# A two-layer mixture-of-experts step: 64 rows per expert in layer 1, with both halves of x in one stationary operand, and w2 loaded in shorter runs

## The chip, the cores and the metric

The kernel runs on one core of one Trainium2 chip. The metric is the device time of one execution in microseconds (us), the median of several.

## What is computed

One inference step of a small streaming encoder: 384 token rows of 1024 (a prompt of 256 and 8 streams of 16) go through two layers. Layer 0 is a gMLP mixer and a mixture of experts, layer 1 latent attention and a mixture of experts. All values are fp32. The change concerns the experts, above all those of layer 1:

```python
def hier_moe(xn, w_group, b_group, w_expert, b_expert, w1, w3, w2):
    ...                                   # top-1 group, top-2 of its 4 experts: gates (384, 16)
    y = jnp.zeros_like(t)
    for e in range(N_EXPERTS):            # 16; w1, w3: 1024 x 512, w2: 512 x 1024
        hdn = jax.nn.silu(t @ w1[e]) * (t @ w3[e])
        y = y + gates[:, e:e + 1] * (hdn @ w2[e])
    return y.reshape(shp)
```

Each row goes to 2 of 16 experts, so an expert has 48 rows on average. With the reference's inputs the fullest has 66 rows in layer 0 and 62 in layer 1.

## The kernel before

**Stages.** gMLP until about 285 us, layer 0's experts from 285 to 553, attention from 553 to 790, layer 1's experts from about 805 to the end. The engines run programs of their own and meet at semaphores; each program is written out by hand, so its order is the code's.

**Rows and passes.** An expert takes CAP = 72 rows. What is over goes to an overflow loop at the end of the layer, of EXTRA = 10 passes that are skipped one by one when there is nothing over; SyncE, GpSimd, ScalarE and TensorE all run through it (`over`, `a.Fori(0, EXTRA)`).

**Precision.** A product of two fp32 operands is made from three: each operand is split into a high part (fp32r, rounded) and a low part (the rest), and high x high, low x high and high x low are summed in PSUM. `split_product` (L181) does so: 16 matmuls (L188) for 8 slices of 128 of the inner dimension, xh and xl in turn against the high part of the weight, then 8 (L194) of xh against its low part. A matmul streams 512 columns of the weight against a stationary slice of x of 128 x 72.

**One round of the loop** (`step`, for expert e; 16 rounds in each layer):

- SyncE loads w1, w3 and w2, 2 MB each, into six raw slots (`load`, L765). Load j of a layer waits until j - 5 weights have been used up (`w_used`). Each is one run of 16 KB in each of 128 partitions, "(p k) n", so slice k of the inner dimension is every 8th (w1, w3) or every 4th (w2) row.
- ScalarE makes a weight's high part (`moe_split_h`, L1079), VectorE the low one in place (`moe_split_l`, L1084).
- TensorE: `product_x` of w1 into bank BA, `transpose_hidden` of expert e - 1 (L1291), `product_x` of w3 into BB, `transpose_x` of the next expert (L1277), `product_y` of expert e - 1 with w2.
- ScalarE: silu of BA (L1133), `hidden_high` of e - 1 (L1100), a split, `x_high` of e + 1 (L1096), a split, `y_copy` of e - 1 (L1118), a split, and the issue of y's store (L1126).
- VectorE: `hidden_low` of e - 1 (L1185), a split, the product hidden = silu x BB (L1200), `x_low` of e + 1 (L1180), two splits. The output of L1200 is read and written by slices, since w2's slices are every 4th row. In layer 1 the table of kept rows (`keep_rows`, L1216 to L1232) comes after round 2 and `kept_columns` (L1236, L1237) after rounds 4 and 15.
- GpSimd fetches the rows of an expert from memory, two ahead (L866); expert 0's and 1's are gathered by TensorE instead (`gather_x`, L1308).

The two halves of x are kept twice (`xsplit`), for the present and the next expert.

Of the kernel before, what the change touches and what calls it, by code (L numbers as in the profile page):

```python
# [29 lines left out]
P = 128  # L30
# [23 lines left out]
CAP = 72  # L54
EXTRA = SLOTS // (CAP + 1)
# [47 lines left out]
def build(nc, A, O):  # L103

    top = ExitStack()
    with top:
# [564 lines left out]
        xsplit = [[sb(f"moe_x{p}{i}", [P, KD, CAP], F32R, moe) for p in "hl"] for i in range(2)]  # L671
# [44 lines left out]
        kept_y = low3[0:CAP, 0:2 * D].rearrange("q (e x n) -> q e x n", e=1, x=2)  # L716
# [13 lines left out]
        silu_done, hid_done = sem("silu_done"), sem("hid_done")  # L730
        hT_done, hh_ready, hl_ready = sem("hT_done"), sem("hh_ready"), sem("hl_ready")
# [27 lines left out]
        def moe_sync(sp, l):  # L759
# [43 lines left out]
            s = over[l]  # L803
# [3 lines left out]
            with sp.Fori(0, EXTRA) as i:  # L807
                with sp.If(n_over > i):
# [7 lines left out]
                    sp.dma_start(rows[0:CAP, 0, :], xrows[bass.ds(row, CAP), :]).then_inc(s["x"], 16)  # L816
# [4 lines left out]
                    sp.dma_start(yrows[bass.ds(row, CAP), :], rows[0:CAP, 2, :]).then_inc(s["st"], 16)  # L821
# [25 lines left out]
        def moe_pool(g, l):  # L847
            if l == 0:
# [67 lines left out]
        def route_vector(v, l):  # L916
            inverse_of_roots(v)
# [1385 lines left out]
```

## Time and profile before

| | |
|---|---|
| median of 3 runs | 1108.43 us (1107.47 to 1110.43) |
| the profiled execution | 1111.0 us, its span 1109.3 us |
| TensorE busy | 1055.8 us, 95% of the span |
| VectorE busy | 780.1 us, 70% |
| ScalarE busy | 595.1 us, 54% |
| DMA | 252 GB/s over the span, 374 to 405 GB/s in most slices of the experts' loops |
| mean granted clock of TensorE | 0.967 |

The chain of work that ended last is TensorE's by 86%, and L188 and L194, the products of the experts, are 46% of it. A granted clock of 1.00 is 2.4 GHz, 0.50 is 1.2 GHz. In a row of the profile, "<-" in square brackets names what ended the wait before an instruction.

### The profile page before, as it was taken

The page shows a single profiled execution, that of the slowest core. Times are in us where ns is not written, and L with a number is a line of the kernel's source. Part 1 is how long each engine was busy: PE and PEld are TensorE (multiplying, and loading weights), DVE is VectorE, ACT ScalarE, POOL GpSimd, SP SyncE. Part 2 cuts the span into 40 slices and gives each one's busy share as a digit, 9 for nine tenths or more (in the row PEclk, how much of TensorE's full clock was granted, in tenths as well). Part 3 has the DMA queues.
Part 4 walks back from the last instruction along what each step waited for, and adds up shares of the span by engine and source line. Part 5 has one row for each costly group of instructions (what it writes and reads, how often), then busy time and mean ns, then how long its engine had stood idle before and what let it go on. Part 6 is the DMA issues. An engine that isn't in the chain of part 4 may idle for free.

```text
span 1109.3 us, 13599 instructions
## 1 busy us (share of the span) xinstructions
PE 1055.8 (95%) x5197; PEld 768.2 (69%) x5197; DVE 780.1 (70%) x629; ACT 595.1 (54%) x462; POOL 84.9 (8%) x109
## 2 busy tenths in 40 slices
PE   5999999999999999999879998889999999999997
PEld 4889998797566666666567767776866666666664
DVE  4447654378698988989354648544678988988886
ACT  5245433253677777777333324232437777777770
POOL 5000000004000000000030020000030000000013
PEclk9999999989999999999989997888899999999999
DMA  9443432756799999997390013005379999999954
GB/s 350 145 162 133 163 128 100 310 240 253 277 396 385 380 400 390 403 387 317 88 337 14 2 39 152 1 1 242 137 287 374 377 387 385 386 402 389 405 198 171
DMA packets 44916, 279.88 MB, mean 252 GB/s; under 512 B 6392, under 2 KB 10904, under 8 KB 32184
## 3 DMA queue, kind: packets, MB, share of 16 engines
q1 hardware_dynamic: 33136, 240.21, 56.1%
q0 software_dynamic: 9216, 30.20, 7.9%
q10 hardware_dynamic: 2520, 8.85, 2.0%
q8 instruction: 32, 0.52, 0.2%
q14 instruction: 12, 0.10, 0.0%
HBM read 260.91 MB, written 18.50 MB: 252 GB/s over the span
## 4 chain that ended last, share of the span: by engine, by line
PE 86%; DVE 7%; ACT 3%; DMA 2%; issue 2%; ACTq 0%; SPq 0%; DVEq 0%
PE ps L188 31%; PE ps L194 15%; PE ps L526 4%; PE ps L580 4%; PE ps L623 3%; PE ps L1972 3%; PE ps L1997 2%; PE ps L586 2%; PE ps L534 2%; PE ps L630 1%; PE ps L1308 1%; PE ps L1068 1%; PE ps L1950 1%; PE ps L1277 1%; DVE moe_wl L1084 1%
## 5 line engine op out<-in xcount | busy, mean ns | idle before, releaser
L1084 DVE TENSOR_TENSOR raw_lo<-raw,moe_wh 128x4096 fp32r<-128x4096 f32 x48 | 212.4, 4425 | 43.9 <-ACT moe_wh L1079 43.9
L1084 DVE TENSOR_TENSOR moe_wl<-moe_raw,moe_wh 128x4096 fp32r<-128x4096 f32 x48 | 212.3, 4424 | 34.3 <-ACT moe_wh L1079 34.1
L188 PE MATMUL ps<-moe_wh,moe_xh 128*72 128x512 f32 x512 | 204.0, 398 | 5.1 <-DVE moe_xl L1180 4.8
L188 PE MATMUL ps<-moe_wh,moe_xl 128*72 128x512 f32 x512 | 202.2, 395 | 0.0
L1079 ACT ACTIVATE moe_wh<-raw 128x4096 fp32r<-128x4096 f32 x48 | 173.8, 3620 | 11.9 <-PE ps L2209 7.6
L1079 ACT ACTIVATE moe_wh<-moe_raw 128x4096 fp32r<-128x4096 f32 x48 | 173.7, 3621 | 4.0 <-DMA moe_raw<-in_moe_w_dram 4.0
L188 PEld LDWEIGHTS ps<-moe_wh,moe_xh 128*72 128x72 f32 x512 | 73.0, 143 | 49.4 <-DVE moe_xl L1180 5.7
L188 PEld LDWEIGHTS ps<-moe_wh,moe_xl 128*72 128x72 f32 x512 | 72.8, 142 | 43.2 <-issue 0.6
L328 DVE TENSOR_TENSOR raw_lo<-raw,gm_wh 128x4096 fp32r<-128x4096 f32 x12 | 53.1, 4425 | 69.7 <-ACT gm_wh L322 67.4
L188 PE MATMUL ps<-moe_wh,moe_hTh 128*72 128x512 f32 x256 | 81.9, 401 | 4.1 <-DVE moe_hTl L1185 3.3
L188 PE MATMUL ps<-moe_wh,moe_hTl 128*72 128x512 f32 x256 | 80.6, 396 | 0.0
L322 ACT ACTIVATE gm_wh<-raw 128x4096 fp32r<-128x4096 f32 x11 | 39.9, 3627 | 57.8 <-DMA raw<-in_gm_w_out_dram 29.1
L194 PE MATMUL ps<-moe_wl,moe_xh 128*72 128x512 f32 x272 | 68.7, 394 | 0.0
L1096 ACT ACTIVATE moe_xh<-ps 128x576 fp32r<-128x576 f32 x32 | 20.9, 652 | 79.7 <-PE ps L1277 53.1
L194 PE MATMUL ps<-raw_lo,moe_xh 128*72 128x512 f32 x240 | 60.6, 394 | 0.0
L1118 ACT ACTIVATE moe_rows<-ps 72x1024 f32<-72x1024 f32 x30 | 30.7, 1023 | 54.9 <-PE ps L194 54.9
L194 PEld LDWEIGHTS ps<-moe_wl,moe_xh 128*72 128x72 f32 x272 | 38.4, 141 | 24.6
L188 PEld LDWEIGHTS ps<-moe_wh,moe_hTl 128*72 128x72 f32 x256 | 36.6, 143 | 23.3 <-issue 0.8
L188 PEld LDWEIGHTS ps<-moe_wh,moe_hTh 128*72 128x72 f32 x256 | 34.3, 143 | 22.5 <-DVE moe_hTl L1185 3.6
L526 PE MATMUL ps<-gm_wh,gm_fx 128*128 128x512 f32 x192 | 46.3, 402 | 2.9 <-ACT gm_wh L315 2.9
L194 PEld LDWEIGHTS ps<-raw_lo,moe_xh 128*72 128x72 f32 x240 | 33.9, 141 | 21.6
L866 POOL DMA_DIRECT2D moe_rows<-moe_xrows x28 | 14.8, 527 | 420.5 <-PE ps L1277 384.9
(391 smaller groups left out, 1647.8 us busy)
## 6 DMA issues: line engine op xcount, KB each, us to landing
raw<-in_moe_w_dram SPq DMA_DIRECT2D x48, 2048.0 KB, 10.9
moe_raw<-in_moe_w_dram SPq DMA_DIRECT2D x48, 2048.0 KB, 11.1
raw<-in_gm_w_in_dram SPq DMA_DIRECT2D x7, 2048.0 KB, 8.0
moe_yrows<-moe_rows ACTq DMA_DIRECT2D x30, 288.0 KB
raw<-in_gm_w_out_dram SPq DMA_DIRECT2D x4, 2048.0 KB, 7.7
moe_rows<-moe_xrows POOLq DMA_DIRECT2D x28, 288.0 KB, 9.7
raw<-in_gm_w_in_dram SPq DMA_DIRECT2D x2, 1024.0 KB, 10.9
at_cache<-in_cache_ckv_dram SPq DMA_DIRECT2D x2, 1024.0 KB, 13.3
```

The costliest lines, as they stand in the source:

```text
L188: nc.tensor.matmul(out[c], x(t, k), wh[:, k, c * 512:c * 512 + 512], start=start and k == 0 and x is xh, stop=False)
L194: last = nc.tensor.matmul(out[c], xh(t, k), wl[:, k, c * 512:c * 512 + 512], start=False, stop=stop and k == nk - 1)
L322: nc.scalar.activation(w_gm[s][:], raw[:, s, :], ACT.Copy).then_inc(wh_ready, 1)
L328: nc.vector.tensor_tensor(raw_lo[:, s, :], raw[:, s, :], w_gm[s][:].bitcast(F32), ALU.subtract).then_inc(wl_ready, 1)
L526: nc.tensor.matmul(ps[:, 3 * (m % 2) + t], x_rows(x, k, t), wh[:, k], start=k == 0 and x is xth, stop=False)
L534: last = nc.tensor.matmul(ps[:, 3 * (m % 2) + t], x_rows(xth, k, t), wl[:, k], start=False, stop=k == KD - 1)
L580: nc.tensor.matmul(ps[:, u_bank(c), 0:TOK], wh[:, k, i * P:(i + 1) * P], x[:, k], start=k == 0 and x is xth, stop=False)
L623: nc.tensor.matmul(ps[:, 2 * t + c], x_rows(x, 4 * j + k, t), wh[:, k, c * 512:c * 512 + 512], start=j == 0 and k == 0 and x is uth, stop= ...
L1079: nc.scalar.activation(w_hi[hi][:], w_raw[slot], ACT.Copy).then_inc(wh_ready, 1)
L1084: nc.vector.tensor_tensor(w_lo[slot], w_raw[slot], w_hi[hi][:].bitcast(F32), ALU.subtract).then_inc(wl_ready, 1)
L1118: nc.scalar.activation(rows[0:CAP, 2 + par].rearrange("p (b n) -> p b n", b=2), ps[0:CAP, BY:BY + 2], ACT.Copy).then_inc(y_out, 1)
L1972: last = nc.tensor.matmul(ps[:, 2 + hp // 2, (hp % 2) * KC:(hp % 2 + 1) * KC], w_uk[:, s, hp * P:(hp + 1) * P], cTs[:, b, s], start=s == 0 ...
```

## The change

Layer 0 still takes 72 rows an expert, layer 1 takes 64, with 11 overflow passes in place of 10 (both layers). In layer 1 the two halves of x stand side by side in one stationary operand of 128 columns, `xwide`, the high half in the first 64, the low half in the other 64. One stacked matmul against the weight's high part does what two did: partitions 0 to 63 of the bank get xh's product, 64 to 127 get xl's. `stacked_product` takes 7 of these, 8 of xh against the low part, and the last stacked one. The two halves of the bank must then be added: ScalarE copies the upper half to SBUF (semaphore `moe_lower`), VectorE adds the lower one to it (`moe_summed`). The silu reads that sum, and the product reads two tiles of SBUF.

w2 is loaded in both layers as "(k p) n", four runs of 4 KB in a partition, and hidden stays in plain order, so L1200's strides are gone. SyncE issues `load_keys_up` (attention's w_uk) ahead of its wait for layer 0's overflow table. The semaphore `at_ms` is folded into `at_red`, with as many waits as before. `cap` replaces CAP wherever a layer's tile is cut.

```diff
-CAP = 72
-EXTRA = SLOTS // (CAP + 1)
+CAPS = (72, 64)
+CAP = max(CAPS)
+EXTRA = SLOTS // (min(CAPS) + 1)
...
+        xs = [sb(f"moe_x{i}", [P, 2 * KD * CAP], F32R, moe) for i in range(2)]
...
+        xwide = [x[:, 0:KD * P].rearrange("p (k t) -> p k t", k=KD) for x in xs]
...
-            return w.rearrange("o (p k) n -> p (o k) n", p=P)
+            return w.rearrange("o (k p) n -> p (o k) n" if name == "moe_w2" else "o (p k) n -> p (o k) n", p=P)
...
+            if l == 0:
+                load_keys_up(sp)
             sp.wait_ge(rt_table, l + 1)
...
             def step(e, par, m):                       # ScalarE
                 a.wait_ge(w_used, M_MOE[l] + (1 if is_first(e) else 3 * e))
                 at_least(a, hid_done, E0 + e)
-                nc.scalar.activation(sil[:], ps[0:CAP, BA], ACT.Silu).then_inc(silu_done, 1)
-                if not is_first(e):
+                if l:
+                    nc.scalar.activation(sil[0:cap], ps[cap:P, BA], ACT.Copy).then_inc(lower, 1)
+                    if not is_first(e):
+                        hidden_high(e - 1)
+                    moe_split_h(a, l, *([3, 0, 3, 0] if is_first(e) else [3 * e + 2, 2, 5 if par else 2, m]))
+                    a.wait_ge(w_used, M_MOE[l] + (2 if is_first(e) else 3 * e + 1))
+                    nc.scalar.activation(hid[0:cap], ps[cap:P, BB], ACT.Copy).then_inc(lower, 1)
+                    a.wait_ge(summed, 2 * e + 1)
+                nc.scalar.activation(sil[0:cap], sil[0:cap] if l else ps[0:cap, BA], ACT.Silu).then_inc(silu_done, 1)
...
             def step(e, par, m):                       # VectorE
+                if l:
+                    v.wait_ge(lower, 2 * e + 1)
+                    nc.vector.tensor_tensor(sil[0:cap], ps[0:cap, BA], sil[0:cap], ALU.add).then_inc(summed, 1)
                 if not is_first(e):
                     hidden_low(e - 1)
...
                 v.wait_ge(w_used, M_MOE[l] + (2 if is_first(e) else 3 * e + 1))
+                if l:
+                    v.wait_ge(lower, 2 * e + 2)
+                    nc.vector.tensor_tensor(hid[0:cap], ps[0:cap, BB], hid[0:cap], ALU.add).then_inc(summed, 1)
+                    v.wait_ge(summed, 2 * e + 2)
                 v.wait_ge(silu_done, E0 + e + 1)
-                nc.vector.tensor_tensor(hid[:].rearrange("q (k p) -> q k p", k=KE), by_slice(sil[:], KE), by_slice(ps[0:CAP, BB], KE),
-                                        ALU.mult).then_inc(hid_done, 1)
+                nc.vector.tensor_tensor(hid[0:cap], sil[0:cap], hid[0:cap] if l else ps[0:cap, BB], ALU.mult).then_inc(hid_done, 1)
...
+            def stacked_product(j, x, xh, wh, wl, bank):
+
+                pe.wait_ge(wh_ready, m0 + j + 2)
+                for k in range(KD - 1):
+                    nc.tensor.matmul(ps[:, bank], x[:, k], wh[:, k], start=k == 0, stop=False)
+                pe.wait_ge(wl_ready, m0 + j + 1)
+                for k in range(KD):
+                    nc.tensor.matmul(ps[0:cap, bank], xh[:, k], wl[:, k], start=False, stop=False)
+                return nc.tensor.matmul(ps[:, bank], x[:, KD - 1], wh[:, KD - 1], start=False, stop=True)
```

The order of VectorE in one round of layer 1 (expert 4), before: moe_hTl is the low part of hidden, raw_lo and moe_wl are low parts of weights, moe_xl that of x, moe_hidden the product.

```order
L1185 TENSOR_TENSOR moe_hTl<-ps,moe_hTh 128x288 [waits hh_ready]
L1084 TENSOR_TENSOR moe_wl<-moe_raw,moe_wh 128x4096 [waits wh_ready]
L1200 TENSOR_TENSOR moe_hidden<-moe_silu,ps 72x512 [waits silu_done,w_used]
L1180 TENSOR_TENSOR moe_xl<-ps,moe_xh 128x576 [waits xh_ready]
L1084 TENSOR_TENSOR moe_wl<-moe_raw,moe_wh 128x4096 [waits wh_ready]
L1084 TENSOR_TENSOR raw_lo<-raw,moe_wh 128x4096 [waits wh_ready]
```

And after, the same round:

```order
L1217 TENSOR_TENSOR moe_silu<-ps,moe_silu 64x512 [waits moe_lower]
L1205 TENSOR_TENSOR moe_hTl<-ps,moe_hTh 128x4x64 [waits hh_ready]
L1092 TENSOR_TENSOR moe_wl<-moe_raw,moe_wh 128x4096 [waits wh_ready]
L1224 TENSOR_TENSOR moe_hidden<-ps,moe_hidden 64x512 [waits moe_lower,w_used]
L1227 TENSOR_TENSOR moe_hidden<-moe_silu,moe_hidden 64x512 [waits silu_done,moe_summed]
L1200 TENSOR_TENSOR moe_x<-ps,moe_x 128x8x64 [waits xh_ready]
L1092 TENSOR_TENSOR moe_wl<-moe_raw,moe_wh 128x4096 [waits wh_ready]
L1092 TENSOR_TENSOR raw_lo<-raw,moe_wh 128x4096 [waits wh_ready]
```

One add has come ahead of hidden_low, one ahead of the product, each with a wait for ScalarE's copy (`moe_lower`).

The order of ScalarE in the same round, before:

```order
L1133 ACTIVATE moe_silu<-ps 72x512 [waits hid_done,w_used]
L1100 ACTIVATE moe_hTh<-ps 128x288 [waits hT_done]
L1079 ACTIVATE moe_wh<-raw 128x4096 [waits w_used,raw_loaded2]
L1096 ACTIVATE moe_xh<-ps 128x576 [waits xT_done]
L1079 ACTIVATE moe_wh<-raw 128x4096 [waits w_used,raw_loaded0]
L1118 ACTIVATE moe_rows<-ps 72x1024 [waits y_stored,w_used]
L1079 ACTIVATE moe_wh<-moe_raw 128x4096 [waits w_used,raw_loaded3]
```

And after, from the first copy (L1145) to the third split:

```order
L1145 ACTIVATE moe_silu<-ps 64x512 [waits hid_done,w_used]
L1111 ACTIVATE moe_hTh<-ps 128x4x64 [waits hT_done]
L1087 ACTIVATE moe_wh<-moe_raw 128x4096 [waits w_used,raw_loaded4]
L1150 ACTIVATE moe_hidden<-ps 64x512 [waits w_used]
L1152 ACTIVATE moe_silu<-moe_silu 64x512 [waits moe_summed]
L1107 ACTIVATE moe_x<-ps 128x8x64 [waits xT_done]
L1087 ACTIVATE moe_wh<-moe_raw 128x4096 [waits w_used,raw_loaded5]
L1129 ACTIVATE moe_rows<-ps 64x1024 [waits y_stored,w_used]
L1087 ACTIVATE moe_wh<-raw 128x4096 [waits w_used,raw_loaded1]
```

The silu (L1152) has moved from ahead of the round's first split to behind it and behind the copy of w3's upper half, and now waits for VectorE's first add.

## Rows read from the trace of the kernel before

**Rows 1.** stretches: start:end, length, busy time by engine, clock, DMA (columns first)
```profile
core 0: us, PE busy (x) PEld busy (x) DVE busy (x) ACT busy (x) POOL busy (x), PEclk, DMA share, GB/s
850.00:1040.00 190.00, 189.22 (x918) 118.95 (x917) 168.66 (x82) 141.98 (x75) 5.71 (x11) 1.00 1.00 389
949.15:966.58 17.43, 17.43 (x86) 10.95 (x84) 15.25 (x7) 13.12 (x7) 0.52 (x1) 1.00 1.01 391
949.00:954.00 5.00, 5.00 (x24) 3.04 (x23) 3.67 (x1) 4.34 (x2) 0.00 (x0) 1.00 0.99 315
954.00:961.00 7.00, 7.00 (x37) 4.44 (x36) 6.15 (x3) 4.61 (x4) 0.00 (x0) 1.00 1.02 433
144.00:148.00 4.00, 4.00 (x26) 4.00 (x25) 3.83 (x6) 1.55 (x2) 0.00 (x0) 1.00 1.00 404
544.76:548.17 3.41, 3.41 (x10) 1.90 (x9) 0.00 (x0) 0.00 (x0) 0.00 (x0) 0.50 0.83 228
581.30:590.00 8.70, 8.70 (x48) 7.74 (x48) 2.26 (x2) 2.18 (x4) 0.00 (x0) 1.00 0.27 72
```

**Rows 2.** chain of waits, layer 1's loop: start us, us, what
```profile
1042.16 0.25 PE ps L1291 x4
1042.41 3.72 PE ps L188 x16
...
1059.57 0.25 PE ps L1291 x4
```

**Rows 3.** landings: expert weights, layer 1; then layer 0; then gMLP output weight
```profile
DMA to landing us min/median/max: 7.4/10.5/11.9
...
DMA to landing us min/median/max: 7.4/11.7/12.9
...
DMA to landing us min/median/max: 7.5/7.7/8.6
```

**Rows 4.** timeline, TensorE, 80 to 140 us: start, us, operation
```profile
82.97 5.67 PE L534 MATMUL ps<-raw_lo,gm_fx 128*128 128x512 f32 x24
```

**Rows 5.** timeline, VectorE, one round of layer 1's loop
```profile
1064.12 4.43 DVE L1084 TENSOR_TENSOR moe_wl<-moe_raw,moe_wh 128x4096 fp32r<-128x4096 f32 x1 [0.61 <-ACT moe_wh L1079]
1068.47 1.08 DVE L1200 TENSOR_TENSOR moe_hidden<-moe_silu,ps 72x512 f32<-72x512 f32 x1
1069.45 0.76 DVE L1180 TENSOR_TENSOR moe_xl<-ps,moe_xh 128x576 fp32r<-128x576 f32 x1
...
1080.40 0.45 DVE L1185 TENSOR_TENSOR moe_hTl<-ps,moe_hTh 128x288 fp32r<-128x288 f32 x1
```

**Rows 6.** groups by line, layer 1's experts: xcount, busy us, mean ns
```profile
L1118 ACT ACTIVATE moe_rows<-ps 72x1024 f32<-72x1024 f32 x14 | 14.3, 1024 | 20.6 <-PE ps L194 20.6
...
L1133 ACT ACTIVATE moe_silu<-ps 72x512 f32<-72x512 f32 x16 | 9.5, 595 | 18.3 <-PE ps L194 18.3
...
L1237 DVE CAST rt_kept_hot<-ps 72x384 fp32r<-72x384 f32 x2 | 1.1, 554 | 0.1
```

**Rows 7.** chain of waits, start of layer 1's experts
```profile
818.80 5.32 PE ps L1308 x48
...
825.65 3.93 PE ps L188 x16
```

**Rows 8.** timeline, VectorE, layer 1, experts 2 and 3
```profile
852.26 0.45 DVE L1185 TENSOR_TENSOR moe_hTl<-ps,moe_hTh 128x288 fp32r<-128x288 f32 x1
...
869.66 0.79 DVE L1216 TENSOR_TENSOR rt_hot<-const,rt_spot 128x216 f32<-128x216 f32 x2
...
872.88 0.46 DVE L1185 TENSOR_TENSOR moe_hTl<-ps,moe_hTh 128x288 fp32r<-128x288 f32 x1 [0.28 <-DVE rt_sent_weight L1232]
```

**Rows 9.** chain of waits, end of layer 0's experts
```profile
555.02 4.13 issue
```

**Rows 10.** timeline, TensorE: two products that waited
```profile
543.94 0.68 PE L188 MATMUL ps<-moe_wh,moe_hTh 128*72 128x512 f32 x2 [2.56 <-DVE moe_hTl L1185]
...
581.26 3.04 PE L1972 MATMUL ps<-at_cache_cT,at_w_uk 128*128 128x256 f32 x13 [1.81 <-ACT at_qa L1769]
```

More of the change, by code:

```diff
@@ L815, in moe_sync @@
                     at_least(sp, s["st"], 16 * i + 16)
-                    sp.dma_start(rows[0:CAP, 0, :], xrows[bass.ds(row, CAP), :]).then_inc(s["x"], 16)
+                    sp.dma_start(rows[0:cap, 0, :], xrows[bass.ds(row, cap), :]).then_inc(s["x"], 16)
                     for slot, name in enumerate(("moe_w1", "moe_w3", "moe_w2")):
@@ L820, in moe_sync @@
                     at_least(sp, s["act"], 5 * i + 5)
-                    sp.dma_start(yrows[bass.ds(row, CAP), :], rows[0:CAP, 2, :]).then_inc(s["st"], 16)
+                    sp.dma_start(yrows[bass.ds(row, cap), :], rows[0:cap, 2, :]).then_inc(s["st"], 16)
             if l == 0:
@@ L865, in load_x @@
                 g.wait_ge(xT_done, NE * l + (2 if isinstance(e, int) and e == 2 else e - 1))
-                g.dma_start(rows[0:CAP, par, :], xrows[bass.ds(row, CAP), :]).then_inc(x_loaded[par], 16)
+                g.dma_start(rows[0:cap, par, :], xrows[bass.ds(row, cap), :]).then_inc(x_loaded[par], 16)
             for e in range(2, 4):
@@ L1125, in store_y @@
                 a.wait_ge(y_out, E0 + e + 1)
-                a.dma_start(yrows[bass.ds(row, CAP), :], rows[0:CAP, 2 + par, :]).then_inc(y_stored, 16)
+                a.dma_start(yrows[bass.ds(row, cap), :], rows[0:cap, 2 + par, :]).then_inc(y_stored, 16)
             x_high(0, 0)
@@ L1307, in gather_x @@
                     for t in range(TILES):
-                        last = nc.tensor.matmul(ps[:, BX + k // 4, (k % 4) * CAP:(k % 4 + 1) * CAP], rows[:, t, k * P:(k + 1) * P],
-                                                hot[:, e, t], start=t == 0, stop=t == TILES - 1)
+                        last = nc.tensor.matmul(ps[:, BX + k // 4, (k % 4) * CAP:(k % 4) * CAP + cap], rows[:, t, k * P:(k + 1) * P],
+                                                hot[:, e, t, 0:cap], start=t == 0, stop=t == TILES - 1)
                 last.then_inc(xT_done, 1)
@@ L1365, in moe_tensor @@
                     for c in range(2):
-                        last = nc.tensor.matmul(ps[:, SPREAD[t][c]], kept_hot[:, 1, t * P:(t + 1) * P].bitcast(F32),
-                                                rows[0:CAP, 3, c * 512:c * 512 + 512], start=False, stop=True)
+                        last = nc.tensor.matmul(ps[:, SPREAD[t][c]], kept_hot[0:cap, 1, t * P:(t + 1) * P].bitcast(F32),
+                                                rows[0:cap, 3, c * 512:c * 512 + 512], start=False, stop=True)
                     last.then_inc(spread, 1)
@@ L1385, in moe_tensor @@
                         for k in range(KD):
-                            last = nc.tensor.matmul(ps[0:CAP, bank], rows[:, 1, k * CAP:(k + 1) * CAP],
+                            last = nc.tensor.matmul(ps[0:cap, bank], rows[:, 1, k * cap:(k + 1) * cap],
                                                     moe_w_view(raw[:, slot], KD)[:, k], start=k == 0, stop=k == KD - 1)
@@ L1396, in moe_tensor @@
                         for k in range(KE):
-                            last = nc.tensor.matmul(ps[0:CAP, BY + c], rows[:, 3, k * CAP:(k + 1) * CAP],
+                            last = nc.tensor.matmul(ps[0:cap, BY + c], rows[:, 3, k * cap:(k + 1) * cap],
                                                     moe_w_view(raw[:, 2], KE)[:, k, c * 512:c * 512 + 512],
```

135 lines of the change are left out of this document (72 added, 63 removed).

## The prediction

> **What bounds the kernel now.** I read first the busy time by stretch, because the change lies almost wholly in layer 1's experts: in their loop TensorE is busy 189.22 of 190.00 us, VectorE 168.66, ScalarE 141.98, and the granted clock is 1.00 [rows 1]. Next the chain of waits there, which says whether a busy engine also sets the pace: it is one unbroken run of TensorE products, 1042.16 to 1059.57, 17.41 us for an expert [rows 2]. In one such round VectorE works 15.25 us and ScalarE 13.12, so a TensorE that gets faster gains only about 1.4 us before VectorE sets the pace, if VectorE got no new work. Then the DMA column: share 1.01 in that round, 391 GB/s [rows 1]. The share cannot tell need from waiting, since a packet also counts while it queues. The landing times can: 7.4 us at best and 10.5 in the median from issue to landing, in a round that needs a load every 17.43 / 3 = 5.81 us [rows 3]. The queue is about two loads deep and stays so; the pace is TensorE's, and the DMA keeps up with little to spare.
>
> **TensorE's saving.** Sixteen high-part products per weight become 8 of 128 stationary columns: 7 + 1 stacked, and the 8 low ones stay. Does a matmul with 128 columns cost more than one with 72? The sixteen of L188 take 3.72 us, 0.2325 each [rows 2]; 24 with a 128-column operand take 5.67, 0.236 each [rows 4]. So the same, and w1 and w3 lose 8 x 0.23 = 1.84 us each: 17.41 - 3.69 = 13.73 us a round, 59 us in 16 experts. That sum is not the forecast, since the round is then VectorE's or the DMA's. The 64 rows save TensorE nothing: the streamed side is 512 wide as before.
>
> **VectorE's round.** Mark a round by the start of hidden_low, L1185, as at 1080.40 [rows 5]. There a split is 4.43 busy, and what follows it starts 0.08 before its end: 4.35 net, three are 13.05. A line through x_low (0.76 for 576 columns) and hidden_low (0.45 for 288) gives 0.69 for 512 and 0.42 for 256, net 0.62 and 0.33: that is x_low and hidden_low after. The two new adds of 512 columns, PSUM + SBUF, are of x_low's kind, 0.62 each. The old multiply, 1.08, reads and writes with a stride; in plain order I take 0.62 net by the same line. Its bounds are 0.47 net, a split's 4.43 us for 4096 columns brought down to 512, and 1.0, no gain from the order. It also waits for the semaphore of the add just ahead of it, some 0.1. Sum 13.05 + 0.62 + 0.33 + 1.24 + 0.62 + 0.1 = **16.0 us**, against 17.41; bounds 15.8 and 16.4.
>
> Two new waits stand in that chain. The first add waits for ScalarE's copy of the upper half of w1's product; behind it on VectorE stand hidden_low and a split, and TensorE's W2 waits for hidden_low. The second add waits for the copy of w3's. I take a copy (512 columns out of PSUM) at the silu's 0.595 [rows 6], same place and size; at worst 1.02, what the 1024-column y copy takes [rows 6]. ScalarE's round is then 13.12 + 2 x 0.595 = 14.3, plus about 0.7 for issuing the y store, 15.0 of 16.0: still below VectorE, and with 1.02 a copy 15.9, where the chains touch and a round costs 0.3 more. silu, which moves behind a split, is ready 1.2 us after W3, just in time for the multiply, whose 0.1 contains it.
>
> **The start.** Before, expert 1's x is gathered 818.80 to 824.12 and its W1 starts at 825.65 [rows 7]; the second mark, T2, is 852.26 [rows 8]. Three products (two of expert 0, W1 of expert 1) shorten by 1.84 each, 5.5; one copy 0.6 and one add 0.62 come in ahead of hidden_low, x_low and the like give back 0.4: gain 4.7, T2 = 847.6.
>
> **If VectorE alone sets it.** From T2 to the mark of the last expert's round, T15 at 1080.40 [rows 5], there are 13 rounds and 228.1 us. After: 13 x 16.0 + 3.2 for keep_rows (869.66 to 872.88, [rows 8]), which is not hidden any more, + 0.7 for kept_columns (0.55 [rows 6] and a small copy) = 211.9. T15 = 1059.5, gain 20.9.
>
> **The DMA's say.** This must be checked, since 2 MB loads have to come every 5.33 us and never came faster than 5.81. Load 8 is issued when the third product of the loop is done, at 828.0 after the change (831.5 before), and lands 7.4 later, 835.4. Load 46, counted from 0, which VectorE's last split before T15 needs, lands 38 loads later, and the split on ScalarE and VectorE plus hidden_low end 8.0 after that. At before's 5.81: 835.4 + 38 x 5.81 + 8.0 = 1064.2, gain **16.2**. The first ten rounds would run at VectorE's pace on data that lies ready, the last three at the DMA's 17.4.
>
> How good is 5.81? Outside the stretch in which a row load runs, the same loop moves 433 GB/s; within it, 315 [rows 1]. The 391 x 17.43 us = 6.8 MB of a round at 433, plus the loss of 5 us at 315 (1.4), are 17.1 us, 5.71 a load, so before's pace may be nearly the DMA's own. Rows of 64 instead of 72 take a ninth off that loss and off the 0.6 MB of rows read and stored, -0.30 a round. w2 in runs of 4 KB: the gMLP's output weight, loaded in such runs, moves 404 GB/s [rows 1] and lands 7.7 us after issue in the median, against 7.4 for the best of the long runs [rows 3]; 2.1 MB at 404 in place of 433 is +0.35 a round. The bounds are nothing (the landings are alike) and 315 GB/s, +1.8 a round. I take +0.35, to which the rate of such a stretch is the nearest row; it and the -0.30 all but cancel, and I keep 5.81, since no row shows a better pace held for a whole round.
>
> By the Trainium skill's page "DMA: Bandwidth & Descriptors", section "Why a DMA increments its semaphore by 16 and not by 1", a hardware-queue transfer is spread over the largest number of engines, up to 16, that divides its outer dimension: 72 rows would go to 12 engines and 64 to all 16. No row here shows the spread of the y stores; by it the loss of the slow stretch would shrink and the sum would lean to the VectorE case.
>
> **The rest.** The last W3 is 1.84 shorter, and a copy and an add stand behind it: -0.5 in the tail. One more pass of the empty overflow loop: ten passes are most of the 4.13 us before attention [rows 9], +0.4. Layer 0 keeps its products and is TensorE's, and its loads land 12.9 us after issue at the latest [rows 3], while ScalarE takes one 18.5 us or more after its issue: 16 x 0.35 = 5.6 of lag just fits, at nothing; what exceeds it costs. Its plain-order multiply shortens a step that nobody waits for. w_uk's earlier issue: it lands long before its use. Overflow passes don't come: no expert of layer 1 gets over 62 rows of the reference's inputs.
>
> Sum: -16.2 - 0.5 + 0.4 = -16.3 on the profiled 1111.0, which is 2.6 over the median; on the median 1108.4 that is **1092.0**.
>
> **Rivals.** *VectorE sets all rounds* (the DMA has room below 5.69 a load, 1051 + 8): -20.9 - 0.1, **1087**. For: 433 GB/s outside the row loads. Against: it never showed a full round faster. *Runs of 4 KB cost dear (slower)*: w2 at the slow stretch's 315 GB/s, +1.8 us an expert, makes both layers the DMA's. Layer 0 loses 15 x 1.8 - 5.6 = 21; in layer 1 a load takes 5.81 - 0.10 + 0.60 = 6.31, T15 is 835.4 + 38 x 6.31 + 8.0 = 1083, 3 later than before: **1133**. It decides from +0.9 a round, where 15 x 0.9 - 5.6 eats the rest's gain, that is below some 365 GB/s; against it speaks the 404 of a stretch with runs of that length.
>
> *The clock falls.* TensorE now idles 16.0 - 13.7 = 2.3 us a round, in gaps of about 1.2 and 0.8 and smaller ones, at hidden_low and at x_low. After an idle of 1.81 it stayed at 1.00, and after one of 2.56 fell to 0.50 [rows 1, 10]. A stretch of 3.4 us at half clock costs 1.7 and fits into the idle time; two a round make 17.1, and only the start is gained: **1103**. By the skill's "TensorE: Matmul & The Clock Gate", section "HAM oscillation — how this bites in real kernels", a wait in each tile can put the engine back to its low clock every time; the trace so far agrees only for the longer wait. *ScalarE's copies are dear*: +0.3 in 13 rounds is 4 on the VectorE case, **1091**, and nothing where the DMA ends last.
>
> **How the numbers follow.** DMA pace 0.50 (1089 to 1098), VectorE's 0.25 (1085 to 1089), clock 0.10 (1098 to 1107), w2 mildly dear, +0.3 to +0.8 a round, 0.08 (1096 to 1105), w2 dear 0.07 (1110 to 1135). The range 1086 to 1103 leaves out some 0.2. Within 0.3% (3.3 us, about what a measurement of this kernel can tell from no change) are the ends of the clock and mild cases, 0.05; slower 0.07; faster 0.88.
>
> **What would show it.** Right: layer 1's rounds 16.0 us with VectorE busy throughout, TensorE 13.7 of them, clock 1.00; late rounds 17.4, ScalarE's split waiting for a raw weight's landing; layer 0 as before. Wrong: a granted clock under 0.9 in the loop, landing times of w2 over 12 us in layer 0, copies near 1 us, or a multiply still at 1.08.

## The result

The changed kernel takes 1092.91 us in the median of four runs (1090.93 to 1097.61), the kernel before 1109.43 beside it (1107.47 to 1111.76): a ratio of 0.985, 95% interval 0.9828 to 0.9872, 14 to 19 us less. Run again later beside other kernels it was 1095.43 (1093.14 to 1096.54) against 1109.33, ratio 0.987 (0.9844 to 0.9895). The forecast was 1092.0 in a range of 1086 to 1103.

The two profiled executions differ by more, 1109.3 and 1091.5 us of span, and part of that is not the change's. The work of expert 0 in layer 1 begins (x_low) at 806.70 before and at 802.48 after:

Chain of waits of the kernel before, at the start of layer 1's experts (start us, us, what):

```profile
806.70 0.77 DVE moe_xl L1180
```

The same of the changed kernel:

```profile
802.48 0.69 DVE moe_x L1200
```

In the twelve other profiles this mark lay anywhere from 801.8 to 807.2, with the same code ahead of it in nearly all. The stretches of attention at half clock lie at other places in them (687 to 697, 711 to 724 and 738 to 748 in the changed kernel, 688 to 702 and 739 to 756 before), which may be why; no run shows it. So I count from this mark to the end of the span, "layer 1" below: 302.6 us before, 289.0 after (288.9 when run again), a gain of 13.6. In the two profiles of the changed kernel it agrees to 0.2 us, where single runs scatter by several.

### The profile page after: what moved, and what is told of

The parts are those of the page before. It is cut to its first block, busy times and chain, and to the rows that moved or that the text cites. A ratio compares the mean times of both kernels' runs of the same rounds, so it can differ in the third digit from the quotient of the medians.

```text
span 1091.5 us, 13229 instructions
## 1 busy us (share of the span) xinstructions
PE 1007.4 (92%) x4941; PEld 739.6 (68%) x4941; DVE 784.3 (72%) x661; ACT 615.5 (56%) x494; POOL 84.2 (8%) x109
## 4 chain that ended last, share of the span: by engine, by line
PE 66%; DVE 14%; DMA 7%; issue 7%; ACT 5%; ACTq 0%; DVEq 0%; SPq 0%
PE ps L189 19%; PE ps L195 9%; DMA raw<-in_moe_w_dram 5%; DVE moe_wl L1092 4%; PE ps L527 4%; PE ps L581 4%; PE ps L624 3%; PE ps L2011 3%; PE ps L2036 3%; ACT moe_wh L1087 2%; PE ps L587 2%; PE ps L535 2%; DVE raw_lo L1092 2%; PE ps L631 2%; PE ps L2239 1%
## 5 line engine op out<-in xcount | busy, mean ns | idle before, releaser
L1087 ACT ACTIVATE moe_wh<-raw 128x4096 fp32r<-128x4096 f32 x48 | 173.8, 3621 | 12.9 <-PE ps L2248 5.1
L189 PE MATMUL ps<-moe_wh,moe_x 128*72 128x512 f32 x512 | 126.9, 401 | 3.1 <-DVE moe_x L1200 2.9
L189 PE MATMUL ps<-moe_wh,moe_hTh 128*72 128x512 f32 (+1 forms) x256 | 83.8, 409 | 27.6 <-DVE moe_hTl L1205 27.0
L189 PEld LDWEIGHTS ps<-moe_wh,moe_x 128*72 128x72 f32 x512 | 72.4, 144 | 47.8 <-DVE moe_x L1200 3.4
L189 PE MATMUL ps<-moe_wh,moe_hTl 128*72 128x512 f32 (+1 forms) x256 | 82.0, 403 | 0.0
L1311 PE MATMUL ps<-moe_wh,moe_x 128*128 128x512 f32 x224 | 60.8, 412 | 10.9 <-DVE moe_x L1200 10.9
L189 PEld LDWEIGHTS ps<-moe_wh,moe_hTh 128*72 128x72 f32 (+1 forms) x256 | 34.0, 143 | 49.2 <-ACT moe_wh L1087 17.0
L1311 PEld LDWEIGHTS ps<-moe_wh,moe_x 128*128 128x128 f32 x224 | 40.5, 192 | 24.4 <-issue 9.8
L189 PEld LDWEIGHTS ps<-moe_wh,moe_hTl 128*72 128x72 f32 (+1 forms) x256 | 36.4, 142 | 25.0 <-issue 2.4
L1107 ACT ACTIVATE moe_x<-ps 128x576 fp32r<-128x576 f32 (+1 forms) x32 | 20.0, 626 | 49.4 <-PE ps L1303 26.9
L527 PEld LDWEIGHTS ps<-gm_wh,gm_fx 128*128 128x128 f32 x192 | 37.6, 198 | 11.3 <-ACT gm_wh L316 3.3
L581 PE MATMUL ps<-gm_fx,gm_wh 128*128 128x384 f32 x256 | 45.2, 335 | 0.0
L581 PEld LDWEIGHTS ps<-gm_fx,gm_wh 128*128 128x128 f32 x256 | 44.3, 188 | 0.1
```

Of the source, the lines that this page charges most:

```text
L189: nc.tensor.matmul(out[c], x(t, k), wh[:, k, c * 512:c * 512 + 512], start=start and k == 0 and x is xh, stop=False)
L527: nc.tensor.matmul(ps[:, 3 * (m % 2) + t], x_rows(x, k, t), wh[:, k], start=k == 0 and x is xth, stop=False)
L581: nc.tensor.matmul(ps[:, u_bank(c), 0:TOK], wh[:, k, i * P:(i + 1) * P], x[:, k], start=k == 0 and x is xth, stop=False)
L1087: nc.scalar.activation(w_hi[hi][:], w_raw[slot], ACT.Copy).then_inc(wh_ready, 1)
L1311: nc.tensor.matmul(ps[:, bank], x[:, k], wh[:, k], start=k == 0, stop=False)
```

## The profile after

By stretch, of the changed kernel (columns in the first line): one round early in the loop, four late ones, and a stretch at its start.

```profile
core 0: us, PE busy (x) PEld busy (x) DVE busy (x) ACT busy (x) POOL busy (x), PEclk, DMA share, GB/s
931.22:947.16 15.94, 14.23 (x68) 9.14 (x68) 15.82 (x9) 14.35 (x10) 0.51 (x1) 1.00 1.01 389
964.38:1031.69 67.31, 56.85 (x272) 36.57 (x272) 63.59 (x33) 58.39 (x37) 1.53 (x3) 1.00 1.02 405
820.03:823.45 3.42, 3.42 (x9) 2.44 (x9) 3.10 (x1) 0.29 (x1) 0.58 (x1) 0.50 0.70 287
```

Beside [rows 1] and [rows 2]: the round is 15.94 us where it was 17.41, and VectorE is busy 15.82 of it, TensorE 14.23. The four late rounds take 67.31, 16.83 each, and there no engine is full: VectorE works 63.59, TensorE 56.85. What fills the rest is a wait of ScalarE for a weight to land. Its timeline (start us, us, operation, idle time before and what ended it):

```profile
943.10 3.62 ACT L1087 ACTIVATE moe_wh<-moe_raw 128x4096 fp32r<-128x4096 f32 x1
...
955.77 3.63 ACT L1087 ACTIVATE moe_wh<-raw 128x4096 fp32r<-128x4096 f32 x1 [1.24 <-DMA raw<-in_moe_w_dram]
...
965.98 3.63 ACT L1087 ACTIVATE moe_wh<-raw 128x4096 fp32r<-128x4096 f32 x1
...
972.57 3.63 ACT L1087 ACTIVATE moe_wh<-moe_raw 128x4096 fp32r<-128x4096 f32 x1 [0.77 <-DMA moe_raw<-in_moe_w_dram]
...
1033.37 3.63 ACT L1087 ACTIVATE moe_wh<-raw 128x4096 fp32r<-128x4096 f32 x1
```

From the split at 943.10 (load 26) to that of load 42, each starts within 0.2 us of its weight's landing. Load 30 is split at 965.98 and load 42 at 1033.37, so a load comes every 67.39 / 12 = 5.62 us. Before, no split of this loop waited for a landing, and a load took 7.4 to 11.9 us to land [rows 3]; now:

```profile
DMA to landing us min/median/max: 10.2/17.3/20.8
```

VectorE's round, its timeline against [rows 5]:

```profile
931.22 0.40 DVE L1205 TENSOR_TENSOR moe_hTl<-ps,moe_hTh 128x256 fp32r<-128x256 f32 x1
931.55 4.40 DVE L1092 TENSOR_TENSOR raw_lo<-raw,moe_wh 128x4096 fp32r<-128x4096 f32 x1
935.89 0.67 DVE L1224 TENSOR_TENSOR moe_hidden<-ps,moe_hidden 64x512 f32<-64x512 f32 x1
936.68 0.68 DVE L1227 TENSOR_TENSOR moe_hidden<-moe_silu,moe_hidden 64x512 f32<-64x512 f32 x1
937.29 0.67 DVE L1200 TENSOR_TENSOR moe_x<-ps,moe_x 128x512 fp32r<-128x512 f32 x1
...
947.16 0.40 DVE L1205 TENSOR_TENSOR moe_hTl<-ps,moe_hTh 128x256 fp32r<-128x256 f32 x1
```

An add, the product and x_low cost alike, 0.67 to 0.68; the product took 1.08 with its stride. Between the second add and the product lie 0.12 us of waiting for the add's semaphore. By line (xcount, busy us, mean ns), the two copies of ScalarE:

```profile
L1145 ACT ACTIVATE moe_silu<-ps 64x512 f32<-64x512 f32 x16 | 9.5, 596 | 10.9 <-PE ps L1315 10.5
L1150 ACT ACTIVATE moe_hidden<-ps 64x512 f32<-64x512 f32 x16 | 9.5, 593 | 0.4
```

## The experiments

Every time below stands beside runs of the kernel before on the same chip; a ratio is to those. "Layer 1" and the rounds are from each kernel's profiled execution.

| kernel | us | ratio to before (95%) | layer 1, us |
|---|---|---|---|
| changed | 1092.9, again 1095.4 | 0.985 (0.983 to 0.987), 0.987 (0.984 to 0.990) | 289.0, 288.9 |
| w2 long, both layers | 1098.2 | 0.988 (0.985 to 0.990) | 295.7 |
| w2 long, layer 1 | 1102.0 | 0.994 (0.991 to 0.996) | 290.1 |
| not stacked | 1110.2 | 0.999 (0.997 to 1.002) | 303.1 |
| half of w2 | 1091.1 | 0.981 (0.977 to 0.984) | 285.9 |
| no adds | 1090.6 | 0.982 (0.977 to 0.988) | 284.3 |
| before, w2 short | 1110.6 | 1.000 (0.998 to 1.002) | 304.2 |
| w1 alone stacked | 1095.0 | 0.986 (0.983 to 0.988) | 288.4 |
| table late | 1102.9 | 0.993 (0.990 to 0.995) | 299.4 |
| warm start | 1095.8 | 0.986 (0.984 to 0.988) | 291.1 |
| table split | 1094.2 | 0.987 (0.985 to 0.990) | 289.4 |
| 72 rows moved | 1100.1 | 0.992 (0.990 to 0.995) | 295.5 |

**What carries the gain.** First the stacking was undone alone (ScalarE's copies and VectorE's adds go with it):

```diff
-                if l:
-                    return stacked_product(j, xwide[par], xh, wh, wl, bank)
                 return split_product(...)
```

> The changed kernel with layer 1's w1 and w3 products as before, 24 matmuls each, without ScalarE's copies and VectorE's adds; 64 rows, w2 in 4 KB runs and the plain order stay. My theory: TensorE's round is 17.4 again and nothing of the gain is left, 1109 us within 3; the loads land 7 us or more ahead of their use. Rival: if 64 rows, the runs of w2 or the plain product carry part of the gain, it stays below 1104.

1110.2 us: all of the gain is gone. By stretch, TensorE is full again:

```profile
830.00:1040.00 210.00, 209.22 (x1019) 126.14 (x1018) 178.55 (x87) 156.36 (x85) 6.12 (x12) 1.00 1.01 386
```

The counterpart puts w2's short runs and the plain order alone into the kernel before:

```diff
-            return w.rearrange("o (p k) n -> p (o k) n", p=P)
+            return w.rearrange("o (k p) n -> p (o k) n" if name == "moe_w2" else "o (p k) n -> p (o k) n", p=P)
```

> The kernel before with only w2's loads in 4 KB runs and the plain order of hidden, in both layers; 72 rows, no stacking. TensorE sets the pace in both loops, so no change, 1110 us, layer 1 from x_low of expert 0 to the end 302 to 303 us as before. If runs of 4 KB were slow for the queue, landing times would climb above the 10.5 (layer 1) and 11.7 us (layer 0) of before by up to 5 us; by the first four experiments, where saturated rounds kept one pace with either run length, they stay within 1 us.

Ratio 0.9998, interval 0.9979 to 1.0018, and landings of 11.0 us in the median in layer 1 and 10.8 in layer 0, against 10.5 and 11.7 [rows 3]. While TensorE sets the pace, neither the runs nor the order nor the 64 rows are worth anything, and the short runs cost nothing: the rival that ended slower is out.

**What ends the rounds now.** Two kernels take away work, one from the DMA and one from VectorE; each leaves out part of the result.

```diff
-                sp.dma_start(moe_w_view(w_raw[slot], ...), w_in_expert(l, name, e))
+                part = slice(0, 2) if l and name == "moe_w2" and not is_last(e) else slice(0, ...)
+                sp.dma_start(moe_w_view(w_raw[slot], ...)[:, part], w_in_expert(l, name, e)[:, part])
```

> The changed kernel, but in layer 1 only half of each expert's w2 (1 MB) is loaded, except the last one; ScalarE splits the loaded half twice and VectorE subtracts the high part from itself, so both engines work as long as before and part of the product is left out. Theory A (DMA ends last from the ninth expert on): with 5 MB a round in place of 6 the loads land early again, every round is VectorE's 15.9, the mark of the last round comes some 7 to 8 us earlier, 1085 to 1087 us. Theory C (VectorE sets all rounds): no change, 1093.

```diff
-                    nc.vector.tensor_tensor(sil[0:cap], ps[0:cap, BA], sil[0:cap], ALU.add).then_inc(summed, 1)
...
-                    nc.vector.tensor_tensor(hid[0:cap], ps[0:cap, BB], hid[0:cap], ALU.add).then_inc(summed, 1)
```

> The changed kernel without VectorE's two adds of a round (the low half's product is left in the place of the sum, so part of the result is left out); ScalarE's copies stay. VectorE's round falls from 15.95 to about 14.7. Theory A (DMA ends last): late rounds stay at 16.8, the lag of the loads only builds up sooner; gain from the start alone, 1 to 3 us, 1090 to 1092. Theory C (VectorE sets the pace): 15 rounds x 1.25 = 19 us, 1074.

VectorE's timeline with half of w2, the marks of three late rounds:

```profile
953.72 0.40 DVE L1215 TENSOR_TENSOR moe_hTl<-ps,moe_hTh 128x256 fp32r<-128x256 f32 x1
969.59 0.41 DVE L1215 TENSOR_TENSOR moe_hTl<-ps,moe_hTh 128x256 fp32r<-128x256 f32 x1
985.53 0.41 DVE L1215 TENSOR_TENSOR moe_hTl<-ps,moe_hTh 128x256 fp32r<-128x256 f32 x1
```

The same without the adds:

```profile
947.55 0.42 DVE L1205 TENSOR_TENSOR moe_hTl<-ps,moe_hTh 128x256 fp32r<-128x256 f32 x1
964.23 0.42 DVE L1205 TENSOR_TENSOR moe_hTl<-ps,moe_hTh 128x256 fp32r<-128x256 f32 x1
980.98 0.42 DVE L1205 TENSOR_TENSOR moe_hTl<-ps,moe_hTh 128x256 fp32r<-128x256 f32 x1
```

With fewer bytes every round from the eighth mark on is VectorE's, 15.87 and 15.94 in turn, and landings fall to 8.0 us in the median. With less work on VectorE the late rounds stay at 16.6 to 17.5, and layer 1 gains 4.8 us, half of that by the second mark, in place of the 19 that VectorE's pace would have given; its last two rounds, which no landing ends, take 15.3. So the loads end the late rounds, and VectorE those early ones that run at full clock. The gain of the kernel with half of w2 is smaller than I had said (3.2 us in layer 1 against 7 to 8): only five rounds of the changed kernel are the DMA's (16.8 to 17.2), each some 1.0 longer than VectorE's, and one early round took 17.3 here, at a granted 0.90, in place of 15.9.

Two early rounds of the changed kernel have a stretch at half clock too, 864 to 881 (17.20 us, behind a wait of 4.06) and 898 to 915. The second, by stretch (columns as above):

```profile
897.90:915.37 17.47, 15.50 (x68) 9.95 (x68) 15.89 (x9) 14.18 (x9) 0.51 (x1) 0.90 1.01 390
```

With w2 long in layer 1 the same round ran at 1.00 and took 15.93. So VectorE's work did not make it longer. What it cost in the end is not shown, since the loads end the late rounds either way.

Stacking w1 alone moves work from VectorE and ScalarE back to TensorE:

```diff
-                if l:
+                if l and bank == BA:
                     return stacked_product(j, xwide[par], xh, wh, wl, bank)
```

> The changed kernel with w1 alone stacked; w3 goes back to 24 matmuls and its copy and add fall away. TensorE 13.73 + 1.84 = 15.6 us a round, VectorE 15.3. If the loads' pace ends the late rounds, they stay at 16.8 and layer 1 lasts 287 to 290 us as with the full change (289.0): 1093 us. If VectorE ended them, rounds would fall to 15.6 and layer 1 to 284.

288.4 us of layer 1, with rounds of 15.9 that no landing ends and late ones of 16.3 to 17.9: as with the full change, as the loads' pace has it.

**What the loads' pace depends on.** First the length of w2's runs, in both layers and in layer 1 alone. The values of hidden stay in plain order; the transposes read them with a stride.

```diff
-            return w.rearrange("o (k p) n -> p (o k) n" if name == "moe_w2" else "o (p k) n -> p (o k) n", p=P)
+            return w.rearrange("o (p k) n -> p (o k) n", p=P)
```

> The changed kernel with w2 back in one run of 16 KB per partition, in both layers; the inner values stay in plain order and the four transposes of hidden read them with a stride instead. VectorE's work is that of the changed kernel. Theory A (the DMA ends last in the loop, and w2's 4 KB runs cost it the 0.35 us a round that the 404 GB/s of such runs say): late rounds fall from 16.8 to about 16.45, load 46 lands 38 x 0.12 = 4.4 us earlier, 1089 us. Theory B (4 KB runs cost nothing): late rounds stay 16.8, 1093. Theory C (VectorE ends last): 1093, rounds 15.9 to 16.0. Slower than 1093 only if the strided transposes cost in layer 0, where TensorE sets the pace.

> The changed kernel with w2 in 16 KB runs in layer 1 alone (layer 0 keeps 4 KB, so its transposes keep plain reads). If run length does not matter to a saturated queue, late rounds are 16.8 to 17.2 and the time 1093; if long runs hold up the scatter and the fetch of rows at the start, as in the run with long w2 in both layers (expert 2's rows 32.6 us after x_low of expert 0, 8 us lost in the first round), then 1097 to 1101.

In the saturated rounds (loads 26 to 42) a load came every 5.62 us with long runs in both layers and every 5.75 with long ones in layer 1, against 5.65 and 5.64 in two profiles with short ones. Long runs don't give a faster queue than short ones. Both kernels are slower than the changed one. For the one with long w2 in both layers the profile shows two other reasons. In layer 0 the strided transposes stand in TensorE's round (268 ns in place of 225, and their operand loads 208 in place of 140): 17.62 us a round in place of 17.40, 2 to 3 us in all. And at the start of layer 1 the rows' way got longer. Chain of waits of this kernel:

```profile
813.31 15.48 DMA moe_xrows<-moe_rows,rt_dst_i
...
830.11 9.60 DMA moe_rows<-moe_xrows
```

GpSimd scatters the rows to memory, waits, and fetches those of expert 2. The scatter's last part landed after 15.5 us here and 16.0 with long runs in layer 1 alone, 12.4 and 12.3 in two profiles of the changed kernel and 12.2 to 12.5 in six others with short runs, with the same two loads beside it, of which one is w2's. (In the kernel before, where both loads were issued after it, it took 10.7 with long runs and 10.9 with short ones.) In the profile shown TensorE then stood 5.60 us before transpose_x of expert 2, and the first round took 26.9 us in place of 18.8; this execution was the slowest of its four, 1104.5 us against 1095.3 to 1099.4, so it over-states the loss. In the profile with long runs in layer 1 alone TensorE did not wait there and layer 1 lasted 290.1, 1.1 longer; that execution was the fastest of its four. What makes the median of this kernel 1102.0 is not shown.

Then the rows. The fetch and the store move 72 rows again, of which 64 are used:

```diff
-                g.dma_start(rows[0:cap, par, :], xrows[bass.ds(row, cap), :])
+                g.dma_start(rows[0:CAP, par, :], xrows[bass.ds(row, CAP), :])
...
-                a.dma_start(yrows[bass.ds(row, cap), :], rows[0:cap, 2 + par, :])
+                a.dma_start(yrows[bass.ds(row, CAP), :], rows[0:CAP, 2 + par, :])
```

> The changed kernel whose fetches of x and stores of y in layer 1 carry 72 rows again, of which 64 are used; all engines' work stays. It measures the prediction's term of 0.30 us a round for the smaller rows, and what the 64 rows do by themselves: in the rounds that the loads end, a load came every 5.65 us (load 26 to load 42 in two profiles). If the term is right, it is 5.75 here, the loads catch up with VectorE two or three rounds sooner and layer 1 lasts 292 to 293 us in place of 289: 1097. If the bytes alone count (0.07 MB a round at some 400 GB/s, 0.16 us), 5.70 and 291. If rows do not matter, 5.65 and 289.

ScalarE's timeline, the splits of loads 30 and 42, both waited for:

```profile
965.84 3.64 ACT L1087 ACTIVATE moe_wh<-raw 128x4096 fp32r<-128x4096 f32 x1 [0.21 <-DMA raw<-in_moe_w_dram]
...
1035.60 3.62 ACT L1087 ACTIVATE moe_wh<-raw 128x4096 fp32r<-128x4096 f32 x1 [0.30 <-DMA raw<-in_moe_w_dram]
```

69.76 / 12 = 5.81 us a load, against 5.62, which would be 0.57 us a round for 16 rows of 4 KB. But that is one profile of each, and kernels that move 64 rows differ almost as much among themselves. The same two splits with w1 alone stacked, both waited for:

```profile
968.72 3.63 ACT L1087 ACTIVATE moe_wh<-raw 128x4096 fp32r<-128x4096 f32 x1 [0.74 <-DMA raw<-in_moe_w_dram]
...
1037.20 3.63 ACT L1087 ACTIVATE moe_wh<-raw 128x4096 fp32r<-128x4096 f32 x1 [0.55 <-DMA raw<-in_moe_w_dram]
```

68.48 / 12 = 5.71, and 5.78 with w2 long in layer 1. By these profiles the rows cost between 0.1 and 0.6 us a round, and the term's 0.30 and the 0.16 of the bytes alone are not told apart. The time itself is clear: 1100.1 us, up to half of the gain lost. In the profile the four rounds from 964 to 1034, at full clock, are 2.7 us longer than those of the changed kernel, and the round ahead of them 0.9 shorter; the other 4.7 of the 6.5 us that layer 1 lost lie in its last two rounds and the tail, where the clock fell in every round:

```profile
1035.00:1070.00 35.00, 31.45 (x138) 20.05 (x137) 31.90 (x17) 28.39 (x18) 5.53 (x2) 0.90 0.70 279
```

Whether the rows bring that about is not shown.

**The start.** In the changed kernel TensorE waits there as follows (timeline of TensorE):

```profile
819.80 3.18 PE L1311 MATMUL ps<-moe_wh,moe_x 128*128 128x512 f32 x7 [3.62 <-DVE moe_x L1200]
...
898.43 1.04 PE L189 MATMUL ps<-moe_wh,moe_hTh 128*64 128x512 f32 x2 [1.69 <-DVE moe_hTl L1205]
```

Seven stacked matmuls of expert 1 take 3.18 us, where seven take 1.8 to 1.9 elsewhere: after 3.62 us of idle time the clock is at 0.50, 820.03 to 823.45 above. One kernel fills the wait:

```diff
                 if f:
                     gather_x(1)
+                    if l:
+                        keep_busy(22)
```

> The changed kernel with 22 idle matmuls of TensorE (256 columns each) behind the gather of expert 1, in the 3.6 us in which it waits for x_low. The clock should stay at 1.00, the first product of expert 1 takes 3.7 us in place of 5.5, and layer 1 gets 1.5 to 2 us shorter, 287: 1091. If the clock's fall there costs nothing, 289.

Timeline of TensorE there, with the clock at 1.00:

```profile
822.81 1.89 PE L1311 MATMUL ps<-moe_wh,moe_x 128*128 128x512 f32 x7 [0.93 <-DVE moe_x L1200]
```

The second mark comes 41.4 us after x_low in place of 42.95, as the clock's price has it, but the time did not improve and layer 1 lasted 291.1 (in the slowest of five executions): it lost the gain again by the last mark, and 1.7 us more in the tail. From 1016 on one stretch of each round ran at half clock, behind a wait of 1.8 to 2.0 us for hidden_low; the rounds of 15.9 have 1.1 there, the late rounds of the changed kernel 2.0 to 2.4 at full clock. By stretch, three of these rounds:

```profile
1016.00:1068.00 52.00, 46.55 (x206) 29.64 (x205) 47.39 (x25) 42.58 (x27) 5.30 (x2) 0.90 0.83 334
```

and VectorE's marks in them:

```profile
1014.59 0.41 DVE L1205 TENSOR_TENSOR moe_hTl<-ps,moe_hTh 128x256 fp32r<-128x256 f32 x1
1032.00 0.41 DVE L1205 TENSOR_TENSOR moe_hTl<-ps,moe_hTh 128x256 fp32r<-128x256 f32 x1
1049.48 0.41 DVE L1205 TENSOR_TENSOR moe_hTl<-ps,moe_hTh 128x256 fp32r<-128x256 f32 x1
```

Rounds of 17.4 and 17.5 at a granted 0.90. The low stretch lay on W2 of the expert before: its 16 matmuls of L189 took 5.3 to 5.5 us in place of 3.7, and ScalarE's y copy, its split and VectorE's third split come after it. The run with 72 rows had the same from 1035 on; the two profiles of the changed kernel had it in single rounds, around 864 and 898, and in the second around 982 and 1016 too.

Two more kernels move the overflow table of layer 1, 5.3 us of VectorE ahead of the first add:

```diff
-            table_vector(v, cap)
+            if l == 0:
+                table_vector(v, cap)
...
-            experts(v, step, {2: keep_rows, 4: lambda: kept_columns(0)} if l else None)
+            experts(v, step, {2: keep_rows, 3: lambda: table_vector(v, cap), 4: lambda: kept_columns(0)} if l else None)
```

> The changed kernel with layer 1's overflow table (5.3 us of VectorE) made after the fourth round in place of before the first. The first add, the product and x_low of expert 1 come 2.3 us sooner, TensorE's wait for them falls from 3.6 to about 1.5 us, its clock does not fall to 0.50 there, and the third product ends 4 us sooner; so does load 8's issue, and by the theory that the loads end the loop at a fixed pace the last mark and layer 1 too: 285 to 286 us, 1089. If VectorE ended the loop, its work is the same in sum and nothing is gained but 1 to 2 us of the clock: 288.

It lost 10 us. The product of expert 1 came 2.0 us sooner against x_low of expert 0, at full clock, and load 8 was issued at 821.1, just ahead of the fetch of expert 2's rows at 821.4; in the changed kernel the fetch comes first, by 3 us, and takes 3.5. Chain of waits of this kernel:

```profile
821.36 9.44 DMA moe_rows<-moe_xrows
...
830.84 1.22 PE ps L1304 x8
```

and its timeline of TensorE:

```profile
830.84 1.22 PE L1304 MATMUL ps<-const,moe_rows 72*128 72x72 f32 x8 [5.80 <-DMA moe_rows<-moe_xrows]
```

So the step that was freed ran into the next wait, and the table, which stands ahead of hidden_low in its new place, made TensorE wait 6.1 us at 886.7, and cost its clock.

```diff
+                if l and is_first(e):
+                    table_vector(v, cap)      # first half
                 x_low(e + 1, 1 - par)
                 if is_first(e):
                     moe_split_l(v, l, 4, 1, 4)
+                    if l:
+                        table_rest(v, cap)    # second half
```

> The changed kernel with layer 1's overflow table in two pieces: the first half (2 us) fills VectorE's wait for the gather of expert 1, between the first product and x_low, the second (3 us) comes after the split behind x_low. Making the table late as a whole lost 10 us, because the rows of expert 2 landed 6 us after TensorE wanted them and VectorE then held up hidden_low for 5.3 us. By the theory that the start is a chain of VectorE's table, x_low of expert 1 and its first product, which runs at half clock after the wait: that product starts at full clock, load 8 is issued 3 to 4 us sooner, layer 1 lasts 286 us, 1090. By the rival that the rows of expert 2 bind next (they land 23.4 us after x_low of expert 0): not more than 1 us, 1092.

The rival's figure held (no gain), but neither reason did. Layer 1 took 289.4, TensorE's wait for x_low was 3.84 us, not shorter, and it did not wait for the rows of expert 2. VectorE's timeline says why:

```profile
807.45 0.68 DVE L1223 TENSOR_TENSOR moe_silu<-ps,moe_silu 64x512 f32<-64x512 f32 x1 [0.40 <-ACT moe_silu L1149]
810.96 4.43 DVE L1096 TENSOR_TENSOR moe_wl<-moe_raw,moe_wh 128x4096 fp32r<-128x4096 f32 x1 [2.83 <-ACT moe_wh L1091]
...
818.80 0.69 DVE L1204 TENSOR_TENSOR moe_x<-ps,moe_x 128x512 fp32r<-128x512 f32 x1
```

VectorE's free time was ahead of the split at 810.96, which waits 2.83 us for ScalarE's, not between the product and x_low, where I put the table. The changed kernel once more, in the same company, was as expected:

> The changed kernel itself once more, beside the two below on the same chip: 1093 us within 2, layer 1 from x_low of expert 0 to the end 289 us within 2, its late rounds 16.8 to 17.2.

1095.4 us, layer 1 288.9. No variant that computes the whole result beat the changed kernel by more than a measurement can tell.

## Why the prediction was right, point by point

**TensorE's saving held.** A stacked matmul costs what the trace of before said for 128 columns [rows 4]: seven take 1.8 to 1.9 us at full clock. TensorE works 14.2 us a round, 0.5 more than forecast, and that ends nothing.

**VectorE's round held to 0.1 us.** 16.0 forecast, 15.85 and 15.94 measured; each new operation lay on the line through x_low and hidden_low [rows 5], and the copies took 0.593 and 0.596 where silu's 0.595 was taken [rows 6]. The round with keep_rows took 18.8 us, 16.0 + 3.2 forecast.

**The loads as the late bound held as a mechanism, with its terms mis-sized.** The forecast kept 5.81 us a load because the smaller rows (-0.30 a round) and the shorter runs (+0.35) would cancel. The shorter runs cost nothing that the runs show, and the smaller rows gave something between 0.1 and 0.6. The saturated queue gave 5.62 to 5.65, late rounds of 16.8 and not 17.4, and five of them, not three. The forecast's own estimate from the rates, 5.71, less 0.10 a load for the rows, is 5.61; what was wrong is the term for the runs, and to hold to 5.81, which was TensorE's pace. The Trainium skill's page "DMA: Bandwidth & Descriptors", section "Why a DMA increments its semaphore by 16 and not by 1", by which 72 rows are spread over 12 engines and 64 over 16 on a hardware queue, leaned the right way. No profile here shows which engines took the rows, and the spread among kernels with 64 rows leaves open whether they cost more than their bytes, so the cause stays open. One sign of being wrong came and meant nothing: from 285 to 512 us loads of layer 0 landed up to 14.4 us after issue (12.9 before), some of w2's among those over 12, but each lay ready 4 us or more ahead of its split, and the rounds stayed at 17.3 to 17.5.

**The start was over-sized.** 4.7 us were forecast up to the second mark (847.6 of before's time). Measured from x_low it came after 42.95 us in place of 45.56 [rows 8], 2.6. The step that failed is the third of the three shortened products: VectorE's table and ScalarE's split made it wait 3.62 us, the clock fell, and it took 5.5 us, as long as before. With the wait filled the mark came at 41.4, a gain of 4.2. The price of a fallen clock stood among the rivals, for the loop and not for the start.

**The sum.** In before's time T15 should have been 1064.2. It was 1063.50 in the profile after, which is 261.0 us after x_low; from before's x_low that is 1067.7. The 3.5 us are: load 8 landed 2.2 us later against x_low (clock at the start, 8.0 us to land in place of 7.4); the 38 loads from there to load 46 took 220.3, against 220.8; and the mark came 9.8 us after load 46's landing, not 8.0, because in the last two rounds VectorE was late again, 15.94 and 15.87. The 38 loads fit by two errors that cancel: up to load 26 a load came only every 6.1 us, in rounds of 15.9 to 18.8 us that no landing ended and of which two were at low clock, then every 5.5. Layer 1 gained 13.6 where 16.7 was forecast (with the tail's 0.9, forecast 0.5). The medians gained 14 to 16.5, so the point of 1092.0 is closer than its parts were: the path was right, but that closeness is luck.

**The extra overflow pass.** The wait before attention, most of which is the loop [rows 9], is 6.89 us on TensorE, and was 6.12: 0.8, forecast 0.4.

**The rival of the clock was under-sized.** Of an idle time alone no rule came out: TensorE fell after 1.69 us at 898.43 above, and stayed at 1.00 after 1.81 before [rows 10] and after longer ones in the changed kernel's late rounds (timeline of TensorE; the clock of 964.38 to 1031.69 above is 1.00):

```profile
964.92 0.68 PE L189 MATMUL ps<-moe_wh,moe_hTh 128*64 128x512 f32 x2 [2.41 <-DVE moe_hTl L1205]
```

I had said that one low stretch a round fits into TensorE's idle time. Two kernels show that it does not where it falls on W2: the round becomes 17.4, because W2 is followed by a chain through ScalarE and VectorE. By the Trainium skill's "TensorE: Matmul & The Clock Gate", section "HAM oscillation — how this bites in real kernels", a wait that recurs in each step can bring the low clock back in each; the rounds at 0.90 agree with that, and the changed kernel's own loop, at 0.98 over 830 to 1040, with two such rounds, shows that the same waits need not do it.

## What to carry to other kernels

When an engine that is 99% busy gets a fifth faster, work out the next two bounds before believing the saving: here 59 us of TensorE time bought about 15, and both bounds could be read from the profile of before, VectorE's round to within 0.1 us and the DMA's to within 0.6. Judge a DMA queue that is "full" by its landing times and by the rate of its best stretch, and take its pace from several profiles before you put a price on a small change beside it: kernels with the same loads and rows differed by 0.16 us a load here. And freeing a step at a stage's start can let a large load slip ahead of a small fetch that somebody waits for; look at what each queue issues next.

## What the runs showed of the hardware that was not expected

- A saturated queue took a load of 2 MB every 5.62 to 5.78 us in kernels that move 64 rows, and every 5.81 in the one that moves 72 (one profile).
- Runs of 4 KB and of 16 KB give a saturated queue the same pace within that spread (5.62 to 5.77 and 5.62 to 5.78 us for 2 MB), but beside a load of w2 in long runs a scatter of rows took 15.5 to 16.0 us to land, beside one in short runs 12.2 to 12.5.
- A fetch of 256 KB landed after 3.5 us ahead of a 2 MB load and after 9.4 right behind its issue.
- An idle time of 1.69 us was followed by half clock, one of 1.81 and one of 2.41 were not; and the low clock came back in each of the last rounds, with a granted mean of 0.90, in two kernels whose rounds wait in the same places as others that stayed at 1.00.
- Transposes whose operand is read with a stride of four elements cost 268 ns in place of 225, and their operand loads 208 in place of 140.
